# Queries and keys transposed in 32x32 blocks by VectorE and re-blocked through DRAM, in place of identity products on TensorE

## The reference, cut to what matters

```
h = rms_norm(x, norm_gain)
proj = einsum('bsd,dn->bsn', h, w_in)        # 13 parts: qa ka va ga qi ki wi qb kb vb gb ma mb
qa, ka: rms_norm per head of 128, then rope  # 8 heads x 128 each
qb, kb: the same                             # 4 heads x 2 maps x 128 each
oa = attention of qa, ka, va over the 64 keys that the indexer (qi, ki, wi) selects
ob = differential attention of qb, kb, vb
x + einsum(sigmoid(ma) * (oa * silu(ga)) @ w_o_a + sigmoid(mb) * (ob * silu(gb)) @ w_o_b, w_out)
```

## Time and profile before

| what | before |
|---|---|
| median of 3 runs | 797.82 us (797.64 to 798.22) |
| span of the profiled execution | 796.4 us, 1.4 less than that median |
| PE busy | 792.7 us (100%), 3810 matmuls |
| DVE busy | 481.5 us (60%) |
| ACT busy | 418.4 us (53%) |
| POOL busy | 46.8 us (6%) |
| DMA | 152.92 MB, mean 192 GB/s |

### The profile page before, as it was taken

The page is one execution under the profiler, slowest core; times in us unless marked ns, Lnnn a source line. Parts: engine busy times, 40 slices in busy tenths (PEclk is TensorE's granted clock), DMA queues, the critical chain, the costliest instruction groups (busy, mean ns, idle before and its releaser), DMA issues.

```text
span 796.4 us, 10773 instructions
## 1 busy us (share of the span) xinstructions
PE 792.7 (100%) x3810; PEld 667.3 (84%) x3810; DVE 481.5 (60%) x663; ACT 418.4 (53%) x670; POOL 46.8 (6%) x70
## 2 busy tenths in 40 slices
PE   9999999999999999999999999999999999999998
PEld 9998888888888888888888888888888888888887
DVE  7677766666677554668656455555455566665453
ACT  7574556665555454556465554555575444443431
POOL 4341000000000000000000000000000000000000
PEclk9999999999999999999999999999999999999999
DMA  9986665666666565666655665655665855555563
GB/s 316 313 264 198 186 187 168 183 199 180 199 187 187 171 194 162 196 189 193 177 154 173 166 176 161 185 160 172 173 185 182 293 195 184 185 194 189 187 194 122
DMA packets 81082, 152.92 MB, mean 192 GB/s; under 512 B 5136, under 2 KB 12944, under 8 KB 80784
## 3 DMA queue, kind: packets, MB, share of 16 engines
q1 hardware_dynamic: 80752, 152.06, 62.8%
q10 hardware_dynamic: 288, 0.30, 0.1%
HBM read 150.25 MB, written 2.10 MB: 191 GB/s over the span
## 4 chain that ended last, share of the span: by engine, by line
PE 97%; ACT 1%; DMA 1%; SPq 0%; issue 0%; DVE 0%; ACTq 0%
PE ps L527 30%; PE ps L529 30%; PE ps L528 29%; PE ps L538 2%; PE ps L569 1%; PE ps L580 1%; DMA raw<-in_w_in 1%; PE ps L638 0%; PE ps L749 0%; PE ps L748 0%; PE ps L747 0%; PE ps L646 0%; ACT L938 0%; ACT L832 0%; ACT g L832 0%; PE ps L626 0%
## 5 line engine op out<-in xcount | busy, mean ns | idle before, releaser
L1068 DVE TENSOR_TENSOR lo<-raw,hi 128x1024 fp32r<-128x1024 f32 (+2 forms) x279 | 335.2, 1204 | 290.2 <-ACT hi L819 288.4
L819 ACT ACTIVATE hi<-raw 128x1024 fp32r<-128x1024 f32 (+2 forms) x277 | 287.1, 1040 | 337.4 <-PE ps L529 323.8
L527 PE MATMUL ps<-hi,hT_hi 128*128 128x512 f32 (+2 forms) x936 | 364.3, 389 | 0.0
L529 PE MATMUL ps<-hi,hT_lo 128*128 128x512 f32 (+2 forms) x936 | 361.1, 386 | 0.0
L528 PE MATMUL ps<-lo,hT_hi 128*128 128x512 f32 (+2 forms) x936 | 360.8, 385 | 0.0
L529 PEld LDWEIGHTS ps<-hi,hT_lo 128*128 128x128 f32 x936 | 175.7, 188 | 35.1
L528 PEld LDWEIGHTS ps<-lo,hT_hi 128*128 128x128 f32 x936 | 175.8, 188 | 32.9
L527 PEld LDWEIGHTS ps<-hi,hT_hi 128*128 128x128 f32 x936 | 175.7, 188 | 33.0
L527 PE MATMUL ps<-hi,ogT_hi 128*128 128x512 f32 x128 | 50.1, 391 | 0.0
L529 PE MATMUL ps<-hi,ogT_lo 128*128 128x512 f32 x128 | 49.8, 389 | 0.0
L528 PE MATMUL ps<-lo,ogT_hi 128*128 128x512 f32 x128 | 49.8, 389 | 0.0
(11 more groups left out here) (167 smaller groups left out, 484.5 us busy)
## 6 DMA issues: line engine op xcount, KB each, us to landing
raw<-in_w_in SPq DMA_DIRECT2D x192, 512.0 KB, 3.8
raw<-in_w_out SPq DMA_DIRECT2D x32, 512.0 KB, 4.3
raw<-in_w_o_a SPq DMA_DIRECT2D x16, 512.0 KB, 3.7
raw<-in_w_o_b SPq DMA_DIRECT2D x16, 512.0 KB, 3.6
raw<-in_w_in SPq DMA_DIRECT2D x13, 384.0 KB, 5.3
raw<-in_w_in SPq DMA_DIRECT2D x8, 336.0 KB, 5.3
x_own<-in_x SPq DMA_DIRECT2D x4, 512.0 KB, 6.4
g<-in_x SPq DMA_DIRECT2D x1, 2048.0 KB, 10.3
```

Of the source, the lines that this page charges most:

```text
L527: mm(o, a_hi, w_hi[:, j], start=first and j == 0, stop=False)
L529: ins = mm(o, a_lo, w_hi[:, j], start=False, stop=j == 1 and last)
L819: activation(hi[:, slot, :, 0:width], raw[:, slot, :, 0:width], ACT.Copy).then_inc(hi_ready, 1)
L1068: tt(lo[:, slot, :, 0:width], raw[:, slot, :, 0:width], hi[:, slot, :, 0:width].bitcast(F32), ALU.subtract).then_inc(lo_ready, 1)
```

## The change

For chunks 3 to 10 PE makes no identity products any more. Instead:

- DVE, at i = 3 of chunk n + 1 and right after the rope's sum: `turn(n)` transposes `roped` in blocks of 32x32 numbers in one instruction over 128x1024 numbers, and writes them into `swapped`. Each block is transposed within its own 32 partitions.
- SP, in its program of loads two chunks later (c = n + 2): after load (c, 3) it waits for `turn(n)` and stores `swapped` (512 KB) into a DRAM buffer, `keep_turned`; after load (c, 4) it waits until that has landed, and reads it back into `roped` in four transfers of 128 KB, `bring_turned`. Each goes to 32 partitions, in pieces of 1 KB, and puts the block rows in their places.
- ACT, `qkT_out(n)` at i = 7 of chunk n + 1, waits until the four reads have landed, and copies out of `roped` in SBUF, no longer out of PSUM; for keys three instructions, not two.
- DVE, `qk_lo_out(n)`: the same sources; for keys two instructions, not one.
- The rope products of the next chunk wait for `qkT_ready` and not for PE.
- SP's loads of chunks 3 to 12 are written out, no longer loops on registers. The indexer's chunks keep their identity products.

```diff
+BLOCK = 32
...
+        turned_home = nc.dram_tensor("turned", (P, RT * CW), F32, kind="Internal").ap()
+        turned_rows = turned_home.rearrange("(q j) (c n) -> c j q n", j=BLOCK, c=P // BLOCK)
+
+        def blocks_of(t):
+            return t[:, :, :].rearrange("p r (b c i) -> p c (r b) i", c=P // BLOCK, i=BLOCK)
+
+        def columns_of(t, r):
+
+            return t[:, :, :].rearrange("p r n -> p (r n)").rearrange("p (q r a b i) -> p r a b q i", q=P // BLOCK, r=RT,
+                                                                      a=2, i=BLOCK)[:, r]
+
+        def by_blocks(t):
+            return t.rearrange("p a b (q i) -> p a b q i", i=BLOCK)
...
-            with sp.Fori(0, 2) as branch:
-                with sp.Fori(0, 4) as n:
-                    load_chunk(C_QK + branch * 4 + n, branch * COL["qb"] + n * CW)
-            for c, name in ((C_V, "va"), (C_V + 2, "vb"), (C_G, "ga"), (C_G + 2, "gb")):
+            def keep_turned(n):
+                sp.wait_ge(qk_turned, n - C_QK + 1)
+                sp.dma_start(turned_home, swapped[:, :, :].rearrange("p r n -> p (r n)")).then_inc(turned_kept, 16)
+
+            def bring_turned(n):
+                sp.wait_ge(turned_kept, 16 * (n - C_QK) + 16)
+                for c in range(P // BLOCK):
+                    to = roped[c * BLOCK:(c + 1) * BLOCK, :, :].rearrange("j r n -> j (r n)")
+                    sp.dma_start(to.rearrange("j (q n) -> j q n", q=P // BLOCK), turned_rows[c]).then_inc(turned_back, 16)
+
+            for c in range(C_QK, C_V + 2):
+                n = c - C_QK
+                col = COL["va"] + (c - C_V) * CW if c >= C_V else n // 4 * COL["qb"] + n % 4 * CW
+                for i in range(CK):
+                    load(i % RING, c * CK + i, w_in, 2 * i, col)
+                    if c >= C_QK + 2 and i == 3:
+                        keep_turned(c - 2)
+                    if c >= C_QK + 2 and i == 4:
+                        bring_turned(c - 2)
+            for c, name in ((C_V + 2, "vb"), (C_G, "ga"), (C_G + 2, "gb")):
...
-                    if c >= 2 and i == 6:
-                        transpose_roped(c - 1, IDX_BLOCKS[c - 1] if c <= C_QK else 4)
+                    if 2 <= c <= C_QK and i == 6:
+                        transpose_roped(c - 1, IDX_BLOCKS[c - 1])
...
-                        if i == 6:
-                            transpose_roped(c - 1)
...
-                    if c == C_V and i == 6:
-                        transpose_roped(C_V - 1)
...
             def qkT_out(n):
 
-                act.wait_ge(qk_transposed, n + 1)
-                four = ps[:, T0:T0 + 2, :].rearrange("p a (b s) -> p a b s", b=2)
+                act.wait_ge(turned_back, 64 * (n - C_QK) + 64)
                 if (n - C_QK) // 2 % 2 == 0:
-                    activation(of_blocks(n, slice(P, S), qk_hi), four[:, :, :, P:S], ACT.Copy)
-                    activation(of_blocks(n, slice(0, P), qkT), four[:, :, :, 0:P], ACT.Copy).then_inc(qkT_ready, 1)
+                    activation(by_blocks(of_blocks(n, slice(P, S), qk_hi)), columns_of(roped, 1), ACT.Copy)
+                    activation(by_blocks(of_blocks(n, slice(0, P), qkT)), columns_of(roped, 0),
+                               ACT.Copy).then_inc(qkT_ready, 1)
                 else:
-                    activation(of_blocks(n, slice(0, S), qk_hi), four, ACT.Copy)
-                    activation(of_four(n, K_FIRST, m), four[:, :, :, 0:P], ACT.Copy).then_inc(qkT_ready, 1)
+                    for r in range(RT):
+                        activation(by_blocks(of_blocks(n, slice(r * P, (r + 1) * P), qk_hi)), columns_of(roped, r), ACT.Copy)
+                    activation(by_blocks(of_four(n, K_FIRST, m)), columns_of(roped, 0), ACT.Copy).then_inc(qkT_ready, 1)
...
-                if 0 in rows and not (isinstance(n, int) and n == 0):
+                if 0 in rows and 0 < n <= C_QK:
                     dve.wait_ge(qk_transposed, n)
+                if 0 in rows and n > C_QK:
+                    dve.wait_ge(qkT_ready, n)
...
+            def turn(n):
+
+                dve.wait_ge(rope_done, n + 1)
+                nc.vector.transpose(swapped[:, :, :].rearrange("p r n -> p (r n)"), blocks_of(roped)).then_inc(qk_turned, 1)
+
...
+                for r, part in ((1, Q_LO),) if (n - C_QK) // 2 % 2 == 0 else enumerate((K_LO_0, K_LO_1)):
+                    ins = tt(by_blocks(of_four(n, part, m_r)), columns_of(roped, r),
+                             by_blocks(of_blocks(n, slice(r * P, (r + 1) * P), qk_hi)).bitcast(F32), ALU.subtract)
+                ins.then_inc(qk_lo_ready, 1)
...
+                    if i == 3:
+                        turn(c - 1)
```

More of the change, by code:

```diff
@@ L190, in build_layer @@
         K_LO, Q_LO, K_FIRST = slice(0, S), slice(S, S + P), slice(S + P, CW)
+        K_LO_0, K_LO_1 = slice(0, P), slice(P, S)
         def of_map(t, part, home):
@@ L310, in build_layer @@
         h_squares, r_h_ready, rope_done = sem("h_squares"), sem("r_h_ready"), sem("rope_done")
+        qk_turned, turned_kept, turned_back = sem("qk_turned"), sem("turned_kept"), sem("turned_back")
         qk_transposed, qkT_ready, qk_lo_ready = sem("qk_transposed"), sem("qkT_ready"), sem("qk_lo_ready")
@@ L558, in w_in_unit, with transpose_roped @@
                     unit(c * CK + i, i % RING, 2 * i, hT_hi, hT_lo, bank, i == 0, i == CK - 1, width)
-            def transpose_roped(n, blocks=4):
+            def transpose_roped(n, blocks):
                 pe.wait_ge(rope_done, n + 1)
-                if not isinstance(n, int) or n > 0:
+                if n > 0:
                     pe.wait_ge(qkT_ready, n)
@@ L569, in transpose_roped @@
                         ins = nc.tensor.transpose(o.bitcast(F32R), roped_r[:, r, b * P:(b + 1) * P], ident_r[:, :])
-                if isinstance(n, int) and n == C_QK - 1:
+                if n == C_QK - 1:
                     for r in range(RT):
@@ L1183, in _ @@
                         norm_rope(c - 1, 0, i - 1)
+                    if c == C_QK + 1 and i == 3:
+                        turn(c - 1)
                     if (c, i) == (2, 1):
@@ L1223, in _ @@
                         norm_rope(c - 1, 3, i - 1)
+                    if c == C_V and i == 3:
+                        turn(c - 1)
                     if c == C_V and i == 7:
```

## The result

The changed kernel takes 844.36 us (median of 4, 843.81 to 844.75) against 797.73 of before: a ratio of 1.0583, with a 95% interval of 1.0569 to 1.0598. 843 was forecast.

What follows compares the result with a forecast made beforehand. TensorE, busy 792.7 of 796.4 us, bounded the kernel before; then the ring would. Delay 8 D - 38.4 = 45.6 us, the 6.0 us of removed products inside it: 797.8 + 45.6 = 843.4 us, range 817 to 868.

Steps and rivals of the forecast that it cites:

- The ring: Transpose, DRAM trip, ScalarE's copies and squares, root, rope, next transpose: binds by 6.4 us a lap; 77 in 100.
- The lap, 17.71 + D: Transpose to next transpose, one per chunk: 17.71 us plus the DRAM trip's 10.5, 28.2 against TensorE's 21.76.
- D: From the end of the lo subtraction to the landing of the last read: 10.5 us, range 7.7 to 12.9.
- The part said to stay: Back-to-back work from the hi copy at 167.21 to the transpose's place at 181.13: unchanged at 13.92 us.
- The sum: First transpose 91.09, seven laps, then the last trip and copies: index scores at 305.4, not 259.82; delay 45.6 us.
- The hidden trip: Rival: the DRAM trip is hidden and TensorE stays the bound, 791.8 us, faster; 3 in 100.
- Trips at their floor: Rival: the ring binds with D at 7.7 or less, slower by less than 23 us, 800 to 821; 8 in 100.
- The dearer transpose: Rival: transpose or read-back dearer than its nearest rows, D + 2.5 or more, over 863 us; 8 in 100.
- The clock: Rival: TensorE's clock falls because it stands before (c+1,3) and (c+1,4); all at 1.2 GHz 966 us; 3 in 100.
- its point of decision: TensorE has 6.4 us per lap to lose; its clock decides only beyond 12.8 us of a lap at 1.2 GHz.
- The share of ports: Reads to 32 partitions reach 8 of 16 ports, about 218 GB/s: D up to 1 us, time 8 us longer.
- my cover of 5 us: Load (c+1,5), held back behind the reads, lands near 12 us after SP's release; ScalarE wants it near 17.

Runs made afterwards that it cites:

- e1: The changed kernel without store and reads, copying straight out of the block-wise transposed tile, block rows not in place: 791.97 us, ratio 0.9921 to before.
- e2: The changed kernel with own places for transpose and reads in the value tile and copies out one chunk later: 791.75 us, ratio 0.9919 to before.
- e4: The changed kernel with VectorE's transpose made twice, the second over the first: 854.85 us, ratio 1.0715 to before.
- e3: The changed kernel with the store one load earlier in SP's program: 842.75 us, ratio 1.0562 to before.
- e7_loads_last: The changed kernel with store and four reads both ahead of loads (c,3) and (c,4) in SP's program: 815.44 us, ratio 1.0219 to before.
- e5: The changed kernel with two of the four reads issued by ScalarE's queue: 841.47 us, ratio 1.0549 to before.
- e8: The changed kernel with filler identity products for TensorE before (c,3), (c,4) and the first index scores: 844.82 us, ratio 1.0575 to before.

## Why the prediction was right, point by point

**The ring.** That the wait closes a ring, and that its length sets the pace, is shown by e1, e2 and e4 together: take the trip out, or the reader out of the ring, and 52 to 53 us are gone; put 1.25 us in at the transpose and 8 x 1.25 come out, and a little more.

**The lap, 17.71 + D.** Predicted 28.2, measured 28.13 over seven. The part said to stay, 13.92 us from hi copy to transpose, is 202.55 - 188.65 = 13.90. The transpose took 1.25 and not 1.14 us. The copies out for keys took 188.65 - 186.98 = 1.67 and not 1.55.

**D.** Predicted 10.5, measured from the end of lo at 176.65 to the landing at 186.96: 10.3. Its two halves erred against each other: the store landed at 182.72 - 176.65 = 6.1 and not 5.75, the reads took 4.2 and not 4.75. That D came out within 0.2 us is in part luck, for two errors cancel. Landings in the views run from the start of an issue (177.08 + 5.64 = 182.72); the sum let them begin at its end, and so had one issue of 0.47 too many in the store and one in the reads. Against that the store itself was put at 4.8 and took 5.64, the median of the earlier trace rows as it stands. The reason for the store's time the forecast had only in part. It counted the load ahead of it, 1.3 us, and missed the second one, (c,4), issued 0.7 us behind it:

```profile
177.10:182.72 5.62, 5.62 (x26) 4.62 (x25) 2.94 (x3) 0.73 (x1) 0.00 (x0) 1.00 0.87 265
```

265 GB/s for 5.62 us are 1.49 MB, moved until the store landed, and the two loads and the store together are 1.57 MB: of the later load, too, at least 0.4 of its 0.52 MB had gone. When I then moved the store, both loads came between it and the reads, and my expectation for e3 fell.

**The sum.** The index scores, foreseen at 305.4, started thus (timeline of PE, changed kernel):

```profile
304.55 0.80 PE L659 MATMUL ps<-g,qkT 64*128 64x128 f32 x4 [8.38 <-ACT v L863]
...
308.44 0.50 PE L562 MATMUL ps<-hi,hT_hi 128*128 128x512 f32 x1
```

304.55 - 259.82 = 44.7 us of delay against the 45.6 forecast. The spans differ by 842.3 - 796.4 = 45.9. The rest is mostly the index scores: with a granted clock of 0.61 they take 308.44 - 304.55 = 3.9 us to the next unit, before 262.33 - 259.82 = 2.5. After that the delay stays as it is. So the span, forecast at 842.0 and measured at 842.3, is nearer than its parts: the delay up to the index scores was forecast 0.9 us too long, and the 1.4 us that they lost at the lower clock were in no term of the sum.

**The rivals.** The hidden trip (791.8 us) is what e2 reached with another place of the reader; in the change as it is it had no chance, with D at 10.3 against 4.05. Trips at their floor: neither was there. The last read took 2.9 us, the middle value of the sum and not 1.9, the store 5.6 and not 2.8. The dearer transpose did not come. The clock did fall, which the rows of before could not say, but it stayed hidden, as its point of decision had it: the mean granted clock of a lap was 1.00 in the first two and 0.88 to 0.94 after them, and 28 x 0.06 = 1.7 us or 29 x 0.12 = 3.5 us of clock are less than the 6.4 to spare. The share of ports named by the Trainium skill for transfers to 32 partitions ("SBUF — State Buffer", "Door 1: The DMA port swizzle") did not show as a loss: four reads of 128 KB needed 4.2 us from first issue to last landing, less than my sum without that rule, and three issues and one landing are most of it. In e7_loads_last there is a stretch with next to nothing but these reads in the DMA engines:

```profile
171.00:172.00 1.00, 1.00 (x6) 0.81 (x5) 0.03 (x1) 0.00 (x0) 0.00 (x0) 1.00 0.91 280
```

280 GB/s is more than the 218 that this page of the Trainium skill gives for 8 ports, so here the four transfers did add up. That is about the pace of their issues, 131 KB every 0.47 us; what they would reach with faster issues no run shows.

**What was off.** TensorE's idle time: 45 us forecast, 222.1 - 187.2 = 34.9 us between 83.9 and 306 by the windows view, 26.4 of them in 20 waits for lo and 8.4 before the index scores. The rest went mostly into slower products. ScalarE's wait for the reads was 6.3 us in the first chunk (6 forecast), then (71.9 - 6.3) / 7 = 9.4 (near 11), since it comes to them later: it also waits for weight loads (34.8 us of waits for raw, outside the path), such as the one that SP issues at 173.14, right after the lo that frees its slot. The load that SP does hold back behind the reads, with my cover of 5 us, is another; it is issued at 184.53, and ScalarE makes its four hi copies from 193.14 on without a wait. That cover held.

## What to carry to other kernels

Before a step is moved off the bounding engine, follow its result to the reader and ask what is queued behind that reader in program order. If the next instance of the step hangs on it, the latency is not paid once but in every lap, and the comparison to make is lap against lap: here 28 us for the ring against 21.8 for TensorE. A faster trip brought 2 to 3 us where other bytes took the gain back (e3, e5) and 29 where the trip got clear of them (e7); only a reader one stage later with a buffer of its own took the whole loss away (e2: 53 us). For each transfer of such a trip the question is which bytes are issued ahead of it and right behind it.

## What the hardware showed that I had not expected

A 512 KB store landed in 5.6 us with one 512 KB load issued 0.4 us before it and another 0.7 after it, in 2.8 with the loads 2.4 us before and 1.1 after it (e3), and in 2.6 with none behind it until it had landed (e7), although at the 404 to 416 GB/s of the earlier trace rows the one ahead is worth 1.3 us. The source view of the store in the changed kernel, and then in e3_store_early, where it goes first:

```profile
L409 SPq DMA_DIRECT2D turned<-swapped x8: 467/467/467, 93.9 to 290.8; - x8
...
DMA to landing us min/median/max: 5.3/5.6/5.7
```

```profile
L409 SPq DMA_DIRECT2D turned<-swapped x8: 338/344/345, 92.1 to 286.2; - x8
...
DMA to landing us min/median/max: 2.8/2.8/3.0
```

The bytes moved until the landing (above, under D) say that the later load took its share too; how much each of the two cost no run separates. And TensorE's granted clock, 1.00 throughout the kernel before, was 0.55 in the 3.8 us after the stand of 3.2 us, and 1.00 again from 195.0 on. With the idle time bridged by identity products, 32 of them in 2.85 us, it stayed at 1.00 in e8's laps but the last, and was 0.58 over the index scores after e8's last stand, 2.8 us without filler.
